# A hybrid attention and pooling layer on 8 cores: attention from the first two token groups on, with all other projections as filling of its steps, tanh gates, and head results in unused storage

## The reference, cut to what matters

```python
z = h @ w_in                                 # (4, 4096, 1024) @ (1024, 3072)
q, k, v = ...                                # 512 columns each: 4 heads, 2 x 64 (q, k), 128 (v)
g_attn, u, g_pool = ...                      # 512 columns each
a = softmax(q1 k1^T / 8) - lam * softmax(q2 k2^T / 8)      # causal
o = rms_norm(a @ v, subln_g) * (1 - lam_init)
attn_out = o * silu(g_attn)
pool_out = (trailing_mean(u, 2 | 4 | 8 | 16) - u) @ w_pool * pool_scale * silu(g_pool)
h = layer_norm(ALPHA * h + concat(attn_out, pool_out) @ w_out)
gate = sigmoid(h @ w_pg + b_pg)
return h + (p @ w_pe) * gate
```

## Time and profile before

| | us |
|---|---|
| median of 3 runs (637.4 to 639.69) | 638.21 |
| the profiled execution | 638.42 |
| its span on the slowest core | 636.9 |
| TensorE busy | 598.9 (94% of the span) |
| VectorE busy | 373.7 (59%) |
| ScalarE busy | 395.7 (62%) |
| GpSimd busy | 164.2 (26%) |

### The profile page before, as it was taken

One profiled execution on the slowest core, in us unless ns is written; L12 is line 12 of the kernel. 1 busy time (PEld: TensorE's weight loads), 2 busy tenths in 40 slices (PEclk: granted clock), 3 DMA queues, 4 the chain that ended last, 5 costly groups with the idle time before them and its releaser, 6 DMA issues.

```text
span 636.9 us, 12686 instructions; the slowest of 8 cores (634.0 to 636.9 us)
## 1 busy us (share of the span) xinstructions
PE 598.9 (94%) x5282; PEld 329.2 (52%) x5282; DVE 373.7 (59%) x733; ACT 395.7 (62%) x609; POOL 164.2 (26%) x160
## 2 busy tenths in 40 slices
PE   6798999999999987999999989899999999999995
PEld 2243444446565643466666654555555556555542
DVE  2215933726766877344434482876676676767894
ACT  2210231348888874587788774577887787887452
POOL 0376930000000000000000000335444444434542
PEclk8999999999999997999999999999999999999998
DMA  8999914040400000130445619301111121123203
GB/s 230 321 293 308 252 22 62 0 58 10 65 4 2 2 2 1 21 47 2 68 67 67 101 15 151 134 2 67 68 67 67 60 74 42 63 69 129 67 34 132
DMA packets 28393, 51.64 MB, mean 81 GB/s; under 512 B 3248, under 2 KB 12848, under 8 KB 28336
## 3 DMA queue, kind: packets, MB, share of 16 engines
q1 hardware_dynamic: 18656, 40.61, 20.4%
q0 software_dynamic: 9680, 10.22, 11.7%
HBM read 52.66 MB, written 8.39 MB: 96 GB/s over the span
## 4 chain that ended last, share of the span: by engine, by line
PE 67%; DVE 9%; ACT 8%; DMA 7%; POOL 4%; SPq 3%; issue 2%; DVEq 0%; ACTq 0%
PE psum_all L540 25%; PE psum_all L860 15%; PE psum_all L827 9%; PE psum_all L748 8%; PE psum_all L681 6%; ACT sb_PT L833 4%; DMA sb_kT<-xT 3%; SPq L154 3%; DMA sb_Vt<-w_in 2%; POOL sb_wsec L430 2%; PE psum_all L784 1%; DMA sb_kT<-w_in 1%; POOL sb_arena L755 1%; DVE sb_PT L843 1%; PE psum_all L726 1%
## 5 line engine op out<-in xcount | busy, mean ns | idle before, releaser
L833 ACT ACTIVATE sb_PT<-psum_all 128x1024 bf16<-128x1024 f32 (+1 forms) x288 | 264.4, 972 | 69.1 <-PE psum_all L827 67.5
L540 PE MATMUL psum_all<-sb_xb,sb_wsec 128*128 128x512 bf16 x640 | 162.5, 383 | 9.6 <-ACT sb_wsec L428 6.5
L860 PEld LDWEIGHTS psum_all<-sb_Vt,sb_PT 128*128 128x128 bf16 x2176 | 133.7, 98 | 32.0 <-DVE sb_PT L843 4.1
L860 PE MATMUL psum_all<-sb_Vt,sb_PT 128*128 128x129 bf16 x2176 | 147.4, 220 | 2.8 <-DVE sb_PT L843 1.9
L540 PE MATMUL psum_all<-sb_wsec,sb_xb 128*128 128x512 bf16 x384 | 96.9, 389 | 6.4 <-DVE sb_arena L595 4.8
L540 PEld LDWEIGHTS psum_all<-sb_xb,sb_wsec 128*128 128x128 bf16 x640 | 56.9, 98 | 75.7 <-issue 18.4
L827 PE MATMUL psum_all<-sb_qT,sb_kT 64*128 64x256 bf16 (+1 forms) x1152 | 89.4, 266 | 4.6 <-ACT sb_PT L833 2.6
L827 PEld LDWEIGHTS psum_all<-sb_qT,sb_kT 64*128 64x128 bf16 x1152 | 42.6, 94 | 73.8 <-ACT sb_PT L833 35.6
L681 PE MATMUL psum_all<-sb_wsec,sb_mixT 128*128 128x512 bf16 x256 | 62.6, 380 | 0.0
L540 PEld LDWEIGHTS psum_all<-sb_wsec,sb_xb 128*128 128x128 bf16 x384 | 34.9, 100 | 47.4 <-issue 7.4
L748 PE MATMUL psum_all<-sb_wsec,sb_arena 128*128 128x512 bf16 x224 | 56.2, 380 | 2.2 <-DVE sb_arena L736 1.8
(11 more groups left out here) (139 smaller groups left out, 629.5 us busy)
## 6 DMA issues: line engine op xcount, KB each, us to landing
sb_Vt<-w_in SPq DMA_DIRECT2D x28, 256.0 KB, 11.7
sb_kT<-w_in SPq DMA_DIRECT2D x20, 256.0 KB, 10.7
sb_Vt<-xT SPq DMA_DIRECT2D x16, 256.0 KB, 11.6
sb_kT<-xT SPq DMA_DIRECT2D x16, 256.0 KB, 12.7
sb_xb<-xT POOLq DMA_DIRECT2D x4, 1024.0 KB, 10.0
sb_xb<-x_own SPq DMA_DIRECT2D x7, 512.0 KB, 3.9
out<-sb_xb SPq DMA_DIRECT2D x7, 512.0 KB, 2.6
sb_wsec<-w_out POOLq DMA_DIRECT2D x2, 1024.0 KB, 11.7
```

Source lines behind the costliest of these rows:

```text
L540: P.op(PE, lambda e: e.matmul(ps[:, bank, :], a, b, start=(kc == 0), stop=(kc == 7)), reads=[B_w[sec], wk[kc], bx, xk[kc]], writes=[B_bank ...
L833: P.op(ACT, lambda e, u=u, pi=pi, q0=q0: e.activation(out=PT[pi][:, :, :, q0:256].rearrange("p k c n -> p c k n"), in_=ps[:, 2 * u:2 * u + ...
L860: P.op(PE, lambda e, u=u, k=k, s=s, kb=kb, qb=qb, c=c, pi=pi, fresh=fresh, done=done: e.matmul(ps[:, BO + qb, c * 130:c * 130 + 129], PT[p ...
```

## The change

- **Start.** The load order becomes w for k, v, then q; attention begins after k and v of groups 0 and 1 and q of group 1, each as four quanta side by side. The constants are loaded ahead of group 2.
- **One stream.** All other projections are feed quanta: `fill0` to `fill3`, one list for each round j. `own(s)`, phA and `block` are gone; `rest_of(s)` puts an own group's gates, halo, the four u in a row, and g and y into the list. The rounds run one after the other. Steps of j=0 carry far more filling than before.
- **take** goes on to a further quantum where 0.6 us or more of the budget are left.
- **Gates** are silu(x) = x (1 + tanh(x/2)) / 2: ScalarE writes tanh to a buffer gt, then VectorE computes (tanh + 1) x out of the bank, which is free only after that. The halves are moved into constants. The sigmoid becomes one Tanh.
- **rms norm**: a GpSimd addition and a GpSimd power take the place of Ln and Exp.
- **Buffers**: head results and gt lie in mixT columns of later rounds, later in qT. Transposes come five steps after the head's last instead of three.
- **Tail**: M of tile 13 is in the hand-written part as a whole.

```diff
         while t < us and self._open():
             d, done = self._one()
             t += d
-            if done:
+            if done and us - t < 0.6:
                 break
...
+        o12 = [View(mfl(i, 3)) for i in range(4)] + [View(qfl(qT[0], h)) for h in (0, 2)]
+        gt = [View(mfl(i, 2)) for i in range(4)] + [View(qfl(qT[1], h)) for h in (0, 2)]
...
+        for kc in range(8):
+            round_(POOL, wsec[0][:, kc, :], fetch(w_src(0, kc)), B_wk[0][kc])
...
         def more_loads():
+            for dst, srcd in ((hl[:], hl_d), (gscb[:], sublng_d.rearrange("d o -> o d").partition_broadcast(128)),
+                              (lamv[:], lamv_d.partition_broadcast(128))):
+                P.dma(SP, dst, srcd, dsc)
+            P.dma(SP, cnt[:], cnt_d, dsc3)
+            P.dma(SP, pscale[:], pscale_d, dsc3)
+            P.dma(POOL, tri3[:].rearrange("p c n -> p (c n)"), tri_d, dsc2)
+            P.dma(POOL, ident[:], ident_d, dsc2)
+            P.dma(POOL, wpool[:], wpool_d.rearrange("(g c) d -> c g d", c=128), dsm)
             for kc in range(8):
                 round_(POOL, xb[0][:, kc, :], fetch(x_src(2, kc)), B_xk[0][kc])
+            for kc in range(8):
+                round_(POOL, wsec[3][:, kc, :], fetch(w_src(3, kc)), B_wk[3][kc])
             xh_v = xh_d.rearrange("(kc p) t -> p kc t", p=128)
             for i in range(4):
                 round_(POOL, xh[:, 2 * i:2 * i + 2, :], fetch(xh_v[:, 2 * i:2 * i + 2, :], 2), B_xh)
-            for kc in range(8):
-                round_(POOL, wsec[4][:, kc, :], fetch(w_src(4, kc)), B_wk[4][kc])
...
-            for s_ in (0, 3):
+            for s_ in (4, 5):
                 for kc in range(8):
                     round_(POOL, wsec[s_][:, kc, :], fetch(w_src(s_, kc)), B_wk[s_][kc])
...
+        def twice_silu(bank, i, out_ap, view, writes):
+            src = ps[:, bank, :].rearrange("p (a n) -> p a n", a=2)
+            P.op(ACT, lambda e: e.activation(out=gt[i][:], in_=src, func=AF.Tanh, scale=0.5), reads=[B_bank[bank]], writes=[B_gt[i]])
+            P.op(DVE, lambda e: e.scalar_tensor_tensor(out=out_ap, in0=view(gt[i][:]), scalar=1.0, in1=view(src), op0=ALU.add, op1=ALU.mult),
+                 reads=[B_gt[i], B_bank[bank]], writes=writes)
...
-                P.op(ACT, lambda e: e.activation(out=z[:], in_=z[:], func=AF.Exp, scale=-1.0), reads=[bz], writes=[bz])
-                P.op(POOL, lambda e: e.tensor_scalar(out=z[:], in0=z[:], scalar1=2.0 ** 62, scalar2=None, op0=ALU.min),
-                     reads=[bz], writes=[bz])
...
-                P.op(ACT, lambda e: e.activation(out=z[:], in_=z[:], func=AF.Ln, bias=1.0, scale=1.0), reads=[bz], writes=[bz])
...
+                P.op(ACT, lambda e: e.activation(out=z[:], in_=z[:], func=AF.Tanh, scale=0.5), reads=[bz], writes=[bz])
...
-            order += [(0, 0, h), (1, 1, h), (0, 1, h), (1, 0, h)]
-        order += [(j, hf, h) for j in (2, 3) for hf in range(2) for h in range(4)]
+            order += [(0, 0, h), (0, 1, h)]
+        order += [(j, hf, h) for j in (1, 2, 3) for hf in range(2) for h in range(4)]
...
-                P.op(ACT, lambda e: e.activation(out=rms, in_=ss, func=AF.Ln, bias=epsb, scale=1.0), reads=[bs, B_eps], writes=[bs])
-                P.op(ACT, lambda e: e.activation(out=rms, in_=rms, func=AF.Exp, scale=-0.5), reads=[bs], writes=[bs])
-                later(2, "mix", mixed)
+                P.op(POOL, lambda e: e.tensor_tensor(out=rms, in0=ss, in1=eps2, op=ALU.add), reads=[bs, B_eps], writes=[bs])
+                P.op(POOL, lambda e: e.tensor_tensor(out=rms, in0=rms, in1=mhalf2, op=ALU.pow), reads=[bs, B_eps], writes=[bs])
+                later(2 if j == 0 else 4, "mix", mixed)
...
+        def rest_of(s):
             u, g, y = q_u(s), q_gp(s), q_y(s)
+            return q_ga(s) + q_halo(s) + u + [g[0], g[1], y[0], g[2], y[1], g[3], y[2], y[3]]
...
         side_by_side(q_k(1), range(4))
-        l0, y0 = own(1)
-        l1, y1 = own(3)
...
-        run_all(phA, [4, 5, 6, 7, 0, 1, 2, 3])
+        side_by_side(q_v(1), range(4, 8))
+        lam_ops()
+        side_by_side(q_q(1), range(4))
...
+        fill0 = q_k(2) + own1[:4] + hooked(q_v(2), lambda: load_xb(4)) + hooked(own1[4:], third_own) + q_k(3) + q_v(3) + q_q(3)
+        fill1 = hooked(own3, lambda: load_xb(5)) + q_k(4) + hooked(q_v(4), lambda: load_xb(6)) + q_k(5) + q_v(5) + q_q(5)
+        fill2 = hooked(own5, lambda: load_xb(7)) + q_k(6) + hooked(q_v(6), load_p) + q_k(7) + hooked(q_v(7), load_wout) + q_q(7)
...
+        fill3 = own7 + fillD
...
-        bounds = {0: (PB, fillB), PB: (PC, fillC), PC: (NS, fillD)}
+        bounds = {0: (P1, fill0), P1: (PB, fill1), PB: (PC, fill2), PC: (NS, fill3)}
...
-                    fins.setdefault(p + 3, []).append(q)
+                    fins.setdefault(p + 5, []).append(q)
```

More of the change, by code:

```diff
@@ L337, in build_nc @@
         flp = lambda t: t[:].rearrange("p k c n -> p (k c n)")
-        gps = [View(flp(PT[i]).bitcast(F32)) for i in range(2)]
         k01 = [f32x2(kT[:, i // 2, (i % 2) * 2048:(i % 2 + 1) * 2048]) for i in range(6)]
@@ L369, in build_nc @@
         B_PT = [Buf() for _ in range(4)]
-        B_g = B_PT[0:2]
+        B_gt, B_psc = [Buf() for _ in range(6)], Buf()
         B_o12 = [Buf() for _ in range(6)]
-        B_rr = [Buf() for _ in range(6)]
         B_sm = [Buf() for _ in range(6)]
@@ L562, in q_q, with next_gt, one, end @@
             return [proj(s, 0, h, lambda bank, h=h: evac(bank, qT[j][:, h, :], [B_q[h][j]], scale=0.125)) for h in range(4)]
+        n_gt = [0]
+        def next_gt(j):
+            n_gt[0] += 1
+            return n_gt[0] % 4 if j < 2 else 4 + n_gt[0] % 2
+        def twice_silu(bank, i, out_ap, view, writes):
[3 more added lines that the diff above has]
+                 reads=[B_gt[i], B_bank[bank]], writes=writes)
         def q_ga(s):
             j = s // 2
[L567 to L575 removed]
+            def one(tb):
+                def end(bank):
+                    t0 = j * GT + tb * 128
+                    made.add(("ga", j, tb))
+                    twice_silu(bank, next_gt(j), mixT[:, 0:4, t0:t0 + 128].rearrange("p (a b) n -> p a b n", a=2),
+                               lambda v: v.rearrange("p a (b n) -> p a b n", b=2), [B_mix[h][j] for h in range(4)])
+                return proj(s, 3, tb, end, swap=True)
+            return [one(tb) for tb in range(4)]
+        held = {}
+        def q_gp(s):
+            def one(p):
+                def end(bank):
+                    i = held[s, p] = next_gt(s // 2)
+                    twice_silu(bank, i, gt[i][:], lambda v: v, [B_gt[i]])
+                return proj(s, 5, p, end)
+            return [one(p) for p in range(4)]
         def q_halo(s):
@@ L769, in end @@
                     made.add(("g", t))
-                    P.op(ACT, lambda e: e.activation(out=z[:, nh, :], in_=ps[:, bank, :], func=AF.Sigmoid),
+                    P.op(ACT, lambda e: e.activation(out=z[:, nh, :], in_=ps[:, bank, :], func=AF.Tanh, scale=0.5),
                          reads=[B_bank[bank], bz], writes=[bz])
@@ L775, in end @@
                 if nh == 1:
-                    after(1, gate1)
+                    after(1, gate)
             return Quantum(([bias] if t >= 12 else []) + [mm(kc) for kc in range(8)], end, (9 if t >= 12 else 8) * MM)
@@ L998, in build_nc, with out_1, out_2, out_3 @@
                 fillD += [q_T(k)]
-        def block(s):
-            ga, gp, y = q_ga(s), q_gp(s), q_y(s)
-            run_all(ga + [gp[0], gp[1], y[0], gp[2], y[1], gp[3], y[2], y[3]], [6, 7, 0, 1, 2, 3])
-            P.op(ACT, lambda e: e.activation(out=sc[:, 8:9], in_=sc[:, 0:1], func=AF.Exp), reads=[B_sc], writes=[B_sc])
-        def start_out():
+        def out_1():
+            olds = list(B_w[3].w.values()) + list(B_w[3].r.values())
+            wload(wpe[:], wpe_d.rearrange("(kc p) n -> p kc n", p=128), [B_w[3]])
+            after(8, lambda: P.op(DVE, lambda e: e.tensor_scalar(out=wpe[:], in0=wpe[:], scalar1=0.5, scalar2=None, op0=ALU.mult),
+                                  reads=[B_w[3]], writes=[B_w[3]]))
+            P.dma(SP, lngb[:].rearrange("p a n -> p (a n)"), lng_d.partition_broadcast(128), dsv, deps=olds)
+        def out_2():
+            olds = list(B_w[5].w.values()) + list(B_w[5].r.values())
+            for dst, srcd in ((lnbb, lnb_d), (bpgb, bpg_d)):
+                P.dma(SP, dst[:].rearrange("p a n -> p (a n)"), srcd.partition_broadcast(128), dsv, deps=olds)
+            t_vec.append((dsv.sem, dsv.cnt))
+        def out_3():
             for i in (1, 2):
@@ L1097, in build_nc @@
         last = steps[NS - 1]
-        M = {(t, nh): q_M(t, nh) for t in (14, 15) for nh in range(2)}
+        M = {(t, nh): q_M(t, nh) for t in (13, 14, 15) for nh in range(2)}
         av(NS - 1)
-        finish_one()
+        feed.drain()
         for p in sorted(fins):
@@ L1110, in build_nc @@
         run("fin_o", "fin_a")
-        for q, b in rest:
-            q.end(b)
-        rest.clear()
```

(17 more changed lines are left out.)

144 lines of the change are left out of this document (46 added, 98 removed).

## The result

The changed kernel takes **687.68 us** (median of 5 runs), the kernel before 638.06 beside it: a ratio of 1.0764, 95% interval 1.0741 to 1.0787. It is slower by 49 us, where I forecast 11.

What follows compares the result with a forecast made beforehand. TensorE, busy 94% of the span, was taken as the bound, so only waits and slow clock could be won. Adds of 24.2 less 13.3 saved gave +10.9 on 638.42: 649 us; terms' range 634 to 660, stated range 626 to 663.

Steps and rivals of the forecast that it cites:

- Saved (b): Blocks 5 and 7: block(5)'s wait and slow clock, 6.4 us, and block(7)'s 1.3 us would be saved.
- adds (e): Later rounds: own group 3 in j=1 adds 3 us (0 to 7); groups 5 and 7 add 1.5 (0 to 5).
- Adds (c): Own group 1 inside j=0: VectorE's chains and products with two banks cost TensorE 12.7 us (8 to 18).
- Adds (f): Gates: a bank is free only after ScalarE and then VectorE, 1 us added (0 to 3).
- Adds (b): First head result, j=0: VectorE waits for GpSimd's rms power behind the roundings, 2 us added (0 to 7).
- Adds (a): Start of attention: q's scaling copies on ScalarE hold banks the first scores need, 1.5 us added (0.5 to 4).
- (d): Added term: `third_own` directly before k of group 3, eight roundings, 2.5 us (0 to 5).
- Saved (a), (c) and (d): Saved waits: weights and halo arriving, 2.8 us; scores behind blocks' last products, 1.5; output-stage exponentials, 1.3.
- Tail, "at nothing": M of tile 13 in the tail counted as no cost; 3.5 us if VectorE's last head result no longer covers it.
- Tables: Rival, some 700 us, chance 0.03: tanh among exponentials needs table loads each way for 44 gates, 113 us on ScalarE.
- Much slower: Rival, 662 us, chance 0.15: full 7 us power wait, own group 1's section at 17, TensorE at 1.2 GHz.
- Faster: Rival, 629 us, chance 0.22: VectorE keeps up in own group 1's section; 13.3 saved against 4 added.

Runs made afterwards that it cites:

- g3: The change with the earlier kernel's first stretch, head order and blocks, and first-round head results finished later: 638.85 us, ratio 0.9991 to the kernel before.
- g5: g3 with blocks 5 and 7 dissolved into the rounds and their u quanta moved ahead among other quanta: 655.25 us, ratio 1.0266 to the kernel before.
- e7: e3 with first-round head results finished later and pooling-gate weight roundings put behind the first two u quanta: 662.85 us, ratio 1.0363 to the kernel before.
- e3: The changed kernel with fillings reordered, u quanta alternating with gate and k or v quanta, nothing left out: 666.09 us, ratio 1.0453 to the kernel before.
- b1: The kernel before with only the u quanta of groups 5 and 7 moved, alternating with v quanta, q last: 646.14 us, ratio 1.0095.
- e1: The changed kernel without VectorE's half of each projection gate, ScalarE's tanh writing straight to the destination: 674.33 us, ratio 1.0576 to the kernel before.
- e5: The changed kernel with x of group 2 loaded ahead of the constants on both DMA queues: 688.17 us, ratio 1.0756 to the kernel before.
- g6: g3 with the last head result's transposes back ahead of tile 15's two quanta: 636.62 us, ratio 0.9967 to the kernel before.
- e8: The changed kernel with 128 unread matmuls added behind group 1's u and pooling gate quanta: 687.27 us, ratio 1.0756 to the kernel before.

## Why the prediction was wrong

The direction held, and the places in part: TensorE idles most in the first round, with banks 6 and 7 released late by gate products and copies, but much of the loss lies in the later rounds, for which I had 4.5 us. The size failed. By the ratios the loss falls into steps, each between two kernels that ran: g3 over before -0.6 us; g5 over g3 (blocks 5 and 7 dissolved, their u spread) 17.5; e7 over g5 (attention from the first two groups, with it the rounds one after the other and groups 1 and 3 in the feed) 6.2; e3 over e7 (power behind the roundings) 5.7; the change over e3 (own groups in a row) 19.8; together 48.7.

- **Saved (b), 6.4 + 1.3: wrong in sign, the first step that failed.** I read the pause at block(5) as what the block costs, and not what it saves. In g3 the block still stands, its wait is 1.3 and its clock full, so most of this saving came without dissolving it; dissolving both blocks costs 17.5, nearly all of it with block(5). From 7.7 saved (with 1.5 of adds (e)) to 17.5 lost is 24 of the 38 us that the forecast was short, though b1 leaves open how much of it is the u quanta's move. The Trainium skill ("Perfetto Trace Analysis", section "Matmul Optimizations") asks for all 8 banks to be used; g3 against g5, six banks against two for the same quanta, agrees in direction; a block also keeps these quanta away from masks and head results, and no run changed the number of banks alone.
- **Adds (e), 3 for group 3 and 1.5 for 5 and 7: the second.** I weighed VectorE's total against TensorE's over 6.4 and 10 steps, 26.6 against 22.3 and 26.6 against 27.5, and called the second a balance. But two banks hold two quanta, 3.5 us of matmuls, and a fourth chain is 4.7, with group 1's small instructions 4.9 (105.47 to 110.39); a mask, a head result and a product behind it add to that. Spreading, with the same sum, gave back 10.2 and 6.1 us in the second and third rounds. So the sums missed the order; that the longest row on VectorE is the measure is how I read it.
- **Adds (c), 12.7: about right, in part by luck.** TensorE idles 40 - 25.3 = 14.7 us from 92 to 132. Without the sums the round ends 10.6 earlier. But the small instructions of the four chains, 4.4 in my sum, took 1.4 here, and VectorE stood 8.7 us for ScalarE's tanh in the same stretch, which I had not put there.
- **Adds (f), 1 (0 to 3): too small.** e1, without VectorE's half of the gate, is 12 us faster; how much of that is the longer hold of the bank, e1 can't say.
- **Adds (b), 2 (0 to 7): the place right, the size at the upper end or past it.** VectorE waited 5.17; doing it later saved 6, by the traces 8.
- **Adds (a), 1.5:** attention began at 49.6, but x of group 2 came late, which the upper end of 4 foresaw; e5 shows that the order of these loads can't simply be turned back. **(d)** does not show as a wait of its own.
- **Saved (a), (c) and (d), 5.6 in all,** were not measured apart; (d)'s edit is in g3, which is even with before.
- **Tail, "at nothing":** it is 3.0 us longer (45.1, before 42.1), near the 3.5 that I named if the cover is gone; g6 shows some 1.1 to 1.5 of it to be the order.
- **Slow clock** had a price only in a rival. In the change it is 0.87 over the first round; e8 brings it back without a gain, but with work added, so that its price stays open there, as in the later rounds.
- **The range.** "634 to 660" does not follow from the terms: their lower ends added up give 634, their upper ends 674 (24.2 of adds become 49). With 687.68 the result is beyond that too.
- **The rivals.** Tables: one load in all, where before had nine, three of them at the attention gates' Silu, so tanh and exponentials do not alternate tables. Eight loads are gone, where saved (e) counts the tail's one; what they cost was not measured. The first row is the change's, the other the largest group of before:

```profile
L427 ACT ACT_TABLE_LOAD x1 | 1.3, 1283 | 1.1 <-PEq L258 1.1
```

```profile
L568 ACT ACT_TABLE_LOAD x3 | 3.8, 1283 | 0.1
```

Much slower: both signs that I gave it came, a wait of 5.17 us for the power and a clock under 1.00 behind it, beside those of my forecast; but its 662 rests on the same saved terms and is 26 us short as well. Faster: I had named VectorE under 85% with TensorE full from 85 to 118 us for it, and over 90% with 10 us of idle TensorE for my forecast. TensorE idles 11.2 of these 33 us, but VectorE is busy 77%; it is nearly full (20.6 of 21.7) only in the row itself:

```profile
85.00:118.00 33.00, 21.76 (x151) 10.26 (x151) 25.47 (x59) 5.71 (x14) 2.75 (x5) 0.79 0.23 33
92.90:114.60 21.70, 12.55 (x85) 5.97 (x83) 20.56 (x49) 4.31 (x9) 0.90 (x2) 0.81 0.34 49
```

A share over a stretch was the wrong test, as in adds (e).
